# Token rows gathered as quarter rows and turned on VectorE in a mixture-of-experts block

## The reference

```
u = rms_norm(x);  proj = u @ w_in
h = x + concat(conv_group(proj), attention(q, k, v)) @ w_out    # 8 heads of 64, 2 key heads, 64-frame chunks
v = rms_norm(h, norm2_g)
logits = v @ router_w + router_b;  gates = softmax(top 4 of 32)
expert(e, v) = act @ w2[e] + b2[e],  act = clamped swiglu of (v @ w1[e] + b1[e])
y = h + sum over the token's 4 experts of gate * expert(e, v)
```

## Time and profile before

| | us |
|---|---|
| median of 3 runs (2012.42 to 2017.47) | 2012.59 |
| the profiled execution | 2012.99 |
| its span | 2011.3 |
| TensorE busy | 1948.9 |
| VectorE busy | 994.6 |
| ScalarE busy | 451.1 |
| GpSimd busy | 227.2 |

### The profile page before, as it was taken

The page is one execution under the profiler, slowest core; times in us unless marked ns, Lnnn a source line. Parts: engine busy times, 40 slices in busy tenths (PEclk is TensorE's granted clock), DMA queues, the critical chain, the costliest instruction groups (busy, mean ns, idle before and its releaser), DMA issues.

```text
span 2011.3 us, 35422 instructions
## 1 busy us (share of the span) xinstructions
PE 1948.9 (97%) x13245; PEld 1617.5 (80%) x13246; DVE 994.6 (49%) x2418; ACT 451.1 (22%) x983; POOL 227.2 (11%) x221
## 2 busy tenths in 40 slices
PE   5999999969999999999999999999999999999997
PEld 3555555438888778888877888999999999999996
DVE  3998972354554544454545454444444444343432
ACT  3265574121111111111111111222122211111111
POOL 3111100010001000101100110111111111100100
PEclk9999999979999999999999999999999999999998
DMA  6000035347999999999999998999888888887652
GB/s 240 1 1 1 24 81 182 133 177 281 330 322 344 335 343 344 341 314 341 345 334 343 343 335 307 316 315 302 295 294 296 299 303 301 287 283 250 215 181 44
DMA packets 233939, 509.08 MB, mean 253 GB/s; under 512 B 7997, under 2 KB 12633, under 8 KB 233888
## 3 DMA queue, kind: packets, MB, share of 16 engines
q1 hardware_dynamic: 215264, 447.97, 62.0%
q0 software_dynamic: 16768, 59.98, 10.8%
q10 hardware_dynamic: 1856, 0.41, 0.1%
HBM read 475.53 MB, written 32.80 MB: 253 GB/s over the span
## 4 chain that ended last, share of the span: by engine, by line
PE 93%; DVE 4%; ACT 1%; issue 1%; POOL 1%; DMA 1%; SPq 0%; ACTq 0%; DVEq 0%; POOLq 0%
PE bank L1138 49%; PE bank L1178 12%; PE bank L1153 12%; PE bank L1371 5%; PE bank L1249 5%; DVE arena L880 2%; PE bank L1517 2%; PE bank L1285 2%; PE bank L1296 1%; PE bank L1322 1%; PE bank L1166 1%; PE bank L1508 1%; PE bank L1167 1%; DMA arena<-in_x 1%; PE bank L1241 0%
## 5 line engine op out<-in xcount | busy, mean ns | idle before, releaser
L1138 PE MATMUL bank<-arena 128*128 128x128 f32 (+5 forms) x8192 | 993.7, 283 | 3.0 <-issue 2.9
L1138 PEld LDWEIGHTS bank<-arena 128*128 128x128 f32 x8192 | 984.9, 191 | 14.3 <-issue 13.7
L769 DVE TENSOR_SCALAR arena<-bank,b1c 128x256 f32<-128x256 f32 x256 | 123.8, 483 | 428.4 <-PE bank L1138 422.8
L469 ACT ACTIVATE arena<-arena 128x256 f32<-128x256 f32 x256 | 106.7, 417 | 849.8 <-DVE arena L769 768.4
L1178 PE MATMUL bank<-arena 128*128 128x512 f32 x576 | 262.1, 593 | 0.0
L1104 DVE TENSOR_SCALAR arena<-bank,cols 128x256 f32<-128x256 f32 x256 | 112.0, 479 | 295.1 <-PE bank L1517 295.1
L1153 PE MATMUL bank<-arena 128*128 128x144 f32 (+4 forms) x1792 | 246.0, 293 | 0.0
L1153 PEld LDWEIGHTS bank<-arena 128*128 128x128 f32 x1792 | 235.9, 190 | 0.1
L357 POOL DMA_INDIRECT out<-arena,idx_cur x64 | 99.0, 1547 | 855.9 <-DVE arena L819 846.1
L880 DVE SCALAR_TENSOR_TENSOR arena<-arena,cols 128x512 f32<-128x512 f32 (+1 forms) x226 | 182.3, 807 | 16.3 <-ACT arena L562 9.3
L1178 PEld LDWEIGHTS bank<-arena 128*128 128x128 f32 x576 | 102.5, 190 | 94.7 <-issue 94.7
(11 more groups left out here) (227 smaller groups left out, 1101.5 us busy)
## 6 DMA issues: line engine op xcount, KB each, us to landing
arena<-in_w SPq DMA_DIRECT2D x192, 2048.0 KB, 12.1
arena<-in_b SPq DMA_DIRECT2D x32, 512.0 KB, 11.0
arena<-in_x SPq DMA_DIRECT2D x16, 512.0 KB, 6.3
token_rows<-arena SPq DMA_DIRECT2D x8, 528.0 KB, 2.9
out<-arena SPq DMA_DIRECT2D x8, 512.0 KB, 6.0
arena<-in_w_in SPq DMA_DIRECT2D x2, 1536.0 KB, 13.0
arena<-in_w_in SPq DMA_DIRECT2D x1, 3072.0 KB, 19.5
arena<-in_w_out SPq DMA_DIRECT2D x1, 2048.0 KB, 7.8
```

What stands on the lines that cost most here:

```text
L469: a.activation(sg[:, m % 2, :], g1[:, m % 2, :], ACT.Sigmoid, scale=ALPHA).then_inc(sg_ready, 1)
L769: v.tensor_scalar(g1[:, r, :], bank[r][:, 0:SLOTS], b1c[:, m:m + 1], LIMIT, ALU.add, ALU.min).then_inc(g1_ready, 1)
L1138: last = mm(bank[m % 2][:, side * SLOTS:side * SLOTS + n], w1_sb[:, k, lo:lo + P], xT[:, k, 0:n], start=k == 0, stop=k == KD - 1)
```

## The change

The normalised row is stored with norm2_g already in it and with its features reordered, so that quarter q of the stored row holds features 32q to 32q+31 of each of the 8 feature blocks. The 32 gates go to a tensor of their own. In the passes, eight indirect DMAs fetch quarter rows of 1 KB: in DMA g, partition 32q + j receives quarter q of the token in slot 32g + j. VectorE then turns 32 x 32 blocks straight into `xT`; `trans_x`, its two PSUM banks' halves and `take_xT` go. The index of a quarter row is 4 x token + q, for which TensorE spreads the 256 token numbers over the partitions with one more float32 matmul of 8 columns per pass. The order of each pass changes with it. The first pass still takes whole rows and is turned by TensorE, after a ScalarE copy that undoes the reordering. The gates come by two more indirect DMAs of 128 rows of 128 bytes (`gather_gates`). In the attention, scores fill two banks at a time with heads of alternating groups. The last token tile's work is reordered, and `norm_v` on VectorE now takes all 8 tiles.

```diff
+BANK_PAIRS = ((0, 2), (1, 3))
-    rows_d = nc.dram_tensor("token_rows", [SEQ, ROW], f32, kind="Internal").ap()
+    rows_d = nc.dram_tensor("token_rows", [SEQ, D], f32, kind="Internal").ap()
+    quads_d = rows_d.rearrange("s (q c) -> (s q) c", q=4)
+    gates_d = nc.dram_tensor("token_gates", [SEQ, NE], f32, kind="Internal").ap()
...
 def store_rows(sp, t):
-            if t == NT - 1:
-                sp.wait_ge(v_ready, 1)
-            sp.dma_start(rows_d[t * P:(t + 1) * P, :], vrow[:, t % 2, :]).then_inc(row_out[t % 2], 16)
+            sp.dma_start(rows_d[t * P:(t + 1) * P, :], vrow[:, t % 2, 0:D]).then_inc(row_out[t % 2], 16)
+            sp.dma_start(gates_d[t * P:(t + 1) * P, :], vrow[:, t % 2, D:]).then_inc(row_out[t % 2], 16)
...
+            sp.dma_start(g2_row, norm2_g.rearrange("(o n) -> o n", o=1).to_broadcast([P, D])).then_inc(g2_in, 16)
...
+        def gather_quads(pool, n):
+            pool.wait_ge(idx_q_ready, n)
+            pool.sem_inc(pool_past, 1)
+            for g in range(8):
+                pool.indirect_dma_start(out=gath_q[:, g, :], out_offset=None, in_=quads_d,
+                                        in_offset=bass.IndirectOffsetOnAxis(ap=idx_q[:, g:g + 1], axis=0)
+                                        ).then_inc(quad_in, 16)
...
             with pool.Fori(0, n_pass) as q:
+                pool.wait_ge(xt_ev, q * 4 + 4)
+                gather_quads(pool, q + 1)
                 pool.wait_ge(cur_ready, q + 1)
-                pool.wait_ge(xt_mm, q * 4 + 4)
-                gather(pool, q + 2)
+                gather_gates(pool)
                 pool.wait_ge(y_ready, q + 1)
...
 def act_pass(a, q, over):
             with a.If(over < 1):
+                sigmoids()
                 take_rows(0)
                 take_rows(1)
             with a.Else():
+                sigmoids()
...
 # ScalarE, before the first pass
+                a.activation(first_tok[:, h, :].rearrange("p (k q r) -> p q k r", k=KD, q=4),
+                             gath[:, h, :].rearrange("p (q k r) -> p q k r", k=KD, q=4), ACT.Copy
+                             ).then_inc(first_tok_ready, 1)
...
 def dve_pass(v, q, e, e_next, prep, one_hots):
+            link(prep(rank[:, :, ds(e_next, 1)].rearrange("p t o -> p (t o)"), baseB[:, ds(q + 1, 1)]))
+            one_hots()
             hidden_a(0)
...
-                if m == 1:
-                    link(prep(rank[:, :, ds(e_next, 1)].rearrange("p t o -> p (t o)"), baseB[:, ds(q + 1, 1)]))
-                    one_hots()
+                if m == 2:
+                    v.wait_ge(idx_mm, q + 2)
+                    link(take_codes(v))
+                    link(take_idx(v, idxf[:]))
+                    link(v.tensor_copy(idx_pass[:], idx_next[:]))
+                    v.wait_ge(gate_in, q * 32 + 32)
+                    v.tensor_copy(idx_next[:], idxf[:]).then_inc(idx_ready, 1)
+                    v.tensor_tensor(spots[:], idxf[:].unsqueeze(2).to_broadcast([P, 2, 4]),
+                                    quad[:].unsqueeze(1).to_broadcast([P, 2, 4]), ALU.mult).then_inc(spots_ready, 1)
                 if m == 3:
+                    v.wait_ge(spread_mm, q + 1)
+                    v.tensor_scalar(idx_q[:], bank[6][:, 16:24], 4.0, quad_id[:], ALU.mult, ALU.add
+                                    ).then_inc(idx_q_ready, 1)
+                if m == 4:
                     for i in range(2):
                         v.wait_ge(added[i], q * 16 + 16)
...
             hidden_b(MT - 1)
-            for i in range(3):
-                take_xT(q4, i)
+            v.wait_ge(quad_in, q * 128 + 128)
+            for g in range(8):
+                ins = v.transpose(xT[:, :, g * 32:(g + 1) * 32], gath_q[:, g, :].rearrange("p (k r) -> p k r", k=KD))
+                if g % 2 == 1:
+                    ins.then_inc(xt_ev, 1)
...
 def norm_v(t):
-                v.tensor_scalar(vrow[:, t % 2, 0:D], hb[:, t % 4, :], rs[:, 2, t:t + 1], None, ALU.mult)
+                for g in range(4):
+                    v.scalar_tensor_tensor(dst[:, g], src[:, g], rs[:, 2, t:t + 1], gain[:, g], ALU.mult, ALU.mult)
...
 # VectorE, last tile
+            residual(NT - 1, (0,))
+            route(NT - 2)
+            residual(NT - 1, (1,))
+            v.wait_ge(lt_mm, NT - 1)
+            v.wait_ge(vt_mm, 2 * NT)
+            v.tensor_copy(vT[:, 4:8, :], bank[5][:].rearrange("p (k q) -> p k q", k=4)).then_inc(vt_ev, 1)
+            norm_v(NT - 1)
+            route(NT - 1)
...
 def pe_pass(pe, q, n, slots_to_tokens):
-                        if m == 0 and side == 0 and k % 2 == 0:
-                            pe.wait_ge(xt_ev, q4 - 3 + k // 2)
+                        if m == 0 and side == 0 and k == 0:
+                            pe.wait_ge(xt_ev, q4)
+                if m == 1:
+                    slots_to_tokens(q + 2)
                 if m == 3:
-                    slots_to_tokens(q + 2)
+                    pe.wait_ge(spots_ready, q + 1)
+                    mm(bank[6][:, 16:24], copies[:], spots[:].rearrange("p h g -> p (h g)"), start=True,
+                       stop=True).then_inc(spread_mm, 1)
...
 def scores(s):
-                for b in range(4):
-                    if s >= 1 and b < 3:
-                        pe.wait_ge(pt_ev, 3 * (s - 1) + b + 1)
-                    if s >= 1 and b == 3:
-                        pe.wait_ge(o_ev, s)
-                    for h in (2 * b, 2 * b + 1):
+                for pair in BANK_PAIRS:
+                    if s >= 1:
+                        if pair == BANK_PAIRS[0]:
+                            pe.wait_ge(pt_ev, 3 * s)
+                        else:
+                            pe.wait_ge(o_ev, s)
+                    for i in range(2):
+                        for b in pair:
+                            g, j = divmod(2 * b + i, GROUP)
...
 # TensorE, last tile
+            out_half(NT - 1, 0)
+            turn_rows(NT - 2)
+            fold_logits(NT - 3)
+            out_half(NT - 1, 1, (0,))
+            logits(NT - 2)
+            out_half(NT - 1, 1, (1,), range(2))
+            turn_rows(NT - 1, (0,))
+            fold_logits(NT - 2)
+            out_half(NT - 1, 1, (1,), range(2, CT))
+            turn_rows(NT - 1, (1,))
+            logits(NT - 1)
```

More of the change, by code:

```diff
@@ L465, in act_pass, with sigmoids @@
             q2 = a.snap(q * 2)
[L466 to L469, removed]
+            def sigmoids():
+                for m in range(MT):
+                    a.wait_ge(g1_ready, q8 + m + 1)
+                    a.wait_ge(sg_free, q8 + m + 1)
+                    a.activation(sg[:, m % 2, :], g1[:, m % 2, :], ACT.Sigmoid, scale=ALPHA).then_inc(sg_ready, 1)
             def take_yT(d):
@@ new lines, in turn_rows @@
+            def turn_rows(u, sides=(0, 1)):
+                if u == 0:
+                    pe.wait_ge(cn_done, 2 * CT)
+                if u == 1:
+                    pe.wait_ge(o_ev, NT)
+                for b in sides:
+                    if u >= 1:
+                        pe.wait_ge(vt_ev, 2 * u)
+                    pe.wait_ge(h_ready if b else h_half, u + 1)
+                    for k in range(4):
+                        c = 4 * b + k
+                        last = pe.transpose(bank[4 + b][:, k * P:(k + 1) * P], hb[:, u % 4, c * P:(c + 1) * P], ident[:])
+                    last.then_inc(vt_mm, 1)
@@ new lines, in logits @@
+            def logits(u):
+                pe.wait_ge(vt_ev, 2 * u + 2)
+                if u >= 1:
+                    pe.wait_ge(lg_neg, u)
+                for j in range(2):
+                    for g in range(4):
+                        last = mm(bank[6][g * NE:(g + 1) * NE, 0:P], rw[:, 4 * j + g, :], vT[:, 4 * j + g, :],
+                                  start=j == 0, stop=j == 1)
+                last.then_inc(lt_mm, 1)
+            for t in range(NT - 1):
+                if t >= 2:
+                    out_half(t, 0)
+                if t >= 1:
+                    turn_rows(t - 1)
+                if t >= 2:
+                    fold_logits(t - 2)
+                if t == 0:
+                    pe.wait_ge(mix_ready, CT)
+                if t == NT // 2:
+                    pe.wait_ge(mix_ready, 2 * CT)
+                out_half(t, 1)
@@ L1473, in _ @@
                     out_half(1, 0, (1,))
-                if 1 <= t <= NT:
-                    u = t - 1
-                    pe.wait_ge(vt_ev, 2 * u + 2)
-                    if u >= 1:
-                        pe.wait_ge(lg_neg, u)
-                    for j in range(2):
-                        for g in range(4):
-                            last = mm(bank[6][g * NE:(g + 1) * NE, 0:P], rw[:, 4 * j + g, :], vT[:, 4 * j + g, :],
-                                      start=j == 0, stop=j == 1)
-                    last.then_inc(lt_mm, 1)
+                else:
+                    logits(t - 1)
                 if t == 1:
@@ L1510, in slots_to_tokens @@
                 last.then_inc(idx_mm, 1)
-            def trans_x(before, i, halves=2):
```

(13 more changed lines are left out.)

218 lines of the change are left out of this document (87 added, 131 removed).

## The result

| | us |
|---|---|
| changed kernel, median of 4 runs (2170.01 to 2175.86) | 2172.84 |
| before, median of 4 runs (2012.42 to 2017.47) | 2014.90 |
| ratio, 95% interval | 1.0784 (1.0771 to 1.0797) |
| profiled execution of the changed kernel, span | 2173.15, 2171.4 |

What follows compares the result with a forecast made beforehand. TensorE was taken as the bound, busy for 97% of the span. Terms -40.9 + 6.9 + 0.4 + 0.3 + 2.7 - 6.0 = -36.6 took 2012.99 to 1976.4 us, 1976 for the median; range 1967 to 1993.

Steps and rivals of the forecast that it cites:

- The quarter gathers: GpSimd's extra gathers and VectorE's transposes in each pass: `xT` complete 5.5 us early, so no cost.
- Rival (d): Quarter rows arrive late and narrow passes wait; at 3.0 us between issues +112, 2088 us; chance 0.05.
- Row transposes and spreading matmul in narrow passes: TensorE in passes: transposes leave, 0.11 us each (-40.9 in all); two new instructions add 0.108 each (+6.9).
- The spots' round trip: VectorE-TensorE-VectorE wait before the spreading matmul: margin 0.7 us, no cost; as a rival +16, 1992 us, chance 0.11.
- DMA (c): DMA traffic in passes: same bytes, more and smaller packets, gates adding 0.4 us, which fits into 2.3 idle.
- rival (c): DMA engines become the bound through 93 ns small packets: +39 over 18 narrow passes, 2015 us; chance 0.10.
- wide passes: TensorE's passes with four row transposes: these take 0.44 us of the chain between down matmuls, all counted as gain.
- Scores: Attention scores: alternating row halves overlap, -0.85 us in each of seven tiles, -6.0 in all.
- rival (a): Score matmuls in the attention don't overlap, so their 6 us gain is lost: 1982 us; chance 0.14.
- Last tile: Last token tile: `norm_v(7)` stands ahead of `route(7)`, which starts at 429.9 instead of 427.16: +2.7 us.
- Constants: VectorE's constants before the convolution: five more short operations, partly inside its waits: +0.3 us, bounds 0 and 1.0.
- The bounds: Lower and upper limits of all the forecast's terms together: said to span 1968 to 1985 us.

Runs made afterwards that it cites:

- e1_pairs: Changed kernel with the eight quarter gathers sent two at a time and the gate gathers held back: 1995.72 us, ratio 0.9903.
- g1_best: Changed kernel, quarter gathers in two rows of four, gate gathers held back, three down-projection banks in wide passes, last-tile row and constants rearranged: 1986.64 us.
- s1: Kernel before with only the alternating order of the scores: 2011.71 us, ratio 0.9988.
- h1: Kernel before with six computing instructions on GpSimd behind the two gathers of each pass: 2016.71 us, ratio 1.0005.
- e4: Kernel before with six more gathers of 32 bytes a row behind the two of each pass: 2051.77 us, ratio 1.0177.
- h2: The kernel of e4 run again, on chip 4, against the kernel before: 2058.47 us, ratio 1.0211.
- r4: The kernel of e8 run again, on chip 5, beside a stalling control: 2240.42 us, ratio 1.1115.
- e8: Changed kernel with each quarter gather fetching for 16 partitions instead of 128, on chip 3: 1990.53 us, ratio 0.9883.
- f2: Changed kernel with the two gate gathers of a pass fetching for 16 partitions instead of 128: 2210.98 us, ratio 1.0974.
- f1: Changed kernel with the two gate gathers behind a wait for TensorE's hidden tile 6 of the pass: 2092.58 us, ratio 1.0383.

## Why the prediction was wrong

**The step that failed** is "The quarter gathers ... Cost of all this: nothing, cover 5.5 us a pass". I counted the six more DMAs and their landing as a deadline for `xT`, and put GpSimd down as an engine that is only late or on time. I did not ask what eight issues in a row do to the others. It is 1720.1 us from the first pass's start to the end in the changed kernel and 1541.1 in e1_pairs (2171.4 - 451.29; 1990.8 - 449.66): **179.0 of the 196.7 us** missed (179.0 here, 13.3 in the passes without the stall, -20.3 for -33.6, and 4.4 ahead of them). Of these 179, TensorE's idle time in the passes is 84 (94.2 against 10.0). The clock was at half for 141 us of the passes instead of 5. TensorE was busy for some 125 of them, so that costs about 60. The rest, some 35, fits matmuls that come singly: 0.27 us for one (782.02 in the changed kernel's chain), where they take 0.11 each in a row. Rival (d), quarters late, had the direction and not the mechanism: the issues stayed 1.24 to 1.33 us apart.

The rest of the steps, read in e1_pairs, where the stall is away:

- **Row transposes and spreading matmul in narrow passes**: 43.69 to 43.03, as forecast. The spreading matmul's 0.22 is 0.12 of its own and 0.10 in the matmuls behind it (14.39 in e1 for the 128 that took 14.29). The spots' round trip cost nothing.
- **DMA (c)**: the traffic cost nothing either, but the count of packets was wrong. The forecast had 1024 packets of 1 KB in the place of 256, and 256 for the gates, so 1024 more a pass; q0 has 5184 more in all, 162 a pass. In the trace the eight quarter gathers of a pass are 256 packets of 4096 bytes. That q0's time grows by the forecast's 0.4 us a pass (10.6% of 2171.4 against 10.8% of 2011.3) is luck, and rival (c), priced by 1024 small packets, had no ground here.
- **In wide passes** I had 16 x 0.11 - 0.22 = -1.5 and got -0.63 to -0.92 (51.31 to 50.55 for 144 slots). The chain of that pass of e1_pairs (L1216 is the down projection, L514 takes its result), against the earlier trace rows:

```profile
1403.65 3.69 PE bank L1216 x30
...
1407.36 0.39 ACT arena L514
...
1407.80 2.23 PE bank L1216 x16
...
1421.62 0.24 issue
1421.87 0.39 PE bank L1197
```

  The transposes had covered ScalarE's taking of a PSUM bank (0.46 of the chain) and the step into the next pass (0.24). I had named no cover for them: some 10 us over 14 passes. In g1_best the third bank removes the first of the two; the same stretch of the next pass, also of 144 slots, is

```profile
1451.29 5.88 PE bank L1235 x48
```

  and that pass takes 50.0 us.
- **The end**: 18.3 us from the last matmul to the end of the span (1972.5 to 1990.8) where it was 15.0 (1996.3 to 2011.3). Of the 3.3 more, 0.5 lie before the last two indirect adds and the rest behind them. No run was made for this, but the traces bear on it. From the last add to the end of the span it is 8.0 to 8.3 us in the kernel before, s1 and h1, and 11.1 to 11.8 with ten gathers of 128 rows a pass. It is 12.3 and 12.9 with the six tiny ones of e4 and h2 added to the two of before, and 8.3 to 9.1 where a pass's quarter or gate gathers were cut to 16 rows (r4, e8, f2). So it hangs on the gathers; how is open.
- **Scores**: -0.85 a tile was forecast. A block's 16 instructions take 1.63 us of the chain instead of 2.25, so -0.62. The tiles of s1, with only the order of the scores changed, are shorter by the same 0.63; its time agrees with -4.4 but can't tell it from much less. An instruction takes 0.10 instead of 0.14, so halves overlap, in part only: rival (a) is out.
- **Last tile**: `route(7)` starts behind `norm_v(7)`, which ends at 428.43 where the route had begun at 427.16, with all before it 1.2 us earlier: +2.5 against +2.7.

```profile
427.16 1.27 DVE arena L1039 x3
428.43 0.24 DVE lg L1044
...
451.29 1.86 PE bank L1192 x7
```

- **Constants**: the first projection block starts at 104.78 instead of 103.83, 0.95 against 0.3. In all, the first pass starts at 451.29 where the forecast of the front gives 446.9 (449.93 + 0.3 + 2.7 - 6.0), 4.4 late. The runs with the same front reach it anywhere from 448.91 (r4) to 454.80 (e8), so this term is no finer than that.
- **The bounds**: taken all one way, those of the terms give 1967 to 1989, not 1968 to 1985.

The rule of "SBUF — State Buffer" in the Trainium skill, that VectorE in a two-port mode can hold up GpSimd's descriptor writing, was not tested. From 771.66 to 773.4 VectorE works without a pause, and the issues beside it are 1.28 to 1.33 us apart, 1.24 to 1.26 without it; but two of these four operations read PSUM and two have two inputs, and no run tells whether any was in such a mode. The harm went another way, from GpSimd's issues to TensorE.

**Left open.** Which path TensorE's signals and instructions share with GpSimd's issues; whether other long work on GpSimd does the same (h1 was too short); and why the runs of chip 3 were free of it, which may be the chip or something else in that session, as the changed kernel itself was not run there. Loading of code by DMA is out: the changed kernel's trace has no packet of the instruction queues (q8, q14) between 495 and 1355 us, where all narrow passes but the first lie. That eight quarter gathers for 16 partitions do more harm than for 128 fits the closer spacing of the issues (1.16 us instead of 1.25), but was not tested apart.

## What to carry to other kernels

Count the indirect DMAs that GpSimd issues in one row, not only their bytes: here, on three of the four chips named, up to four at a time beside a dense float32 matmul stream were free and eight cost 4 us a pass; waits that split the row of ten were worth 8%. When "issue" stands as the reason for a TensorE gap and the next engine's idle says "remote", look at what GpSimd does at that time. And before taking filler out of a bound engine's queue, look which waits it had covered.

## What was not expected of the hardware

- TensorE's signals reached VectorE up to 6.5 us late in a row of 8 to 10 indirect DMA issues (f2_gates16), up to 8.3 with quarter gathers of 16 rows (r4_rows16), and GpSimd too (2.56 us idle in f1); otherwise 0.04 us behind the last matmul.
- TensorE went on with hidden matmuls for 8.3 us from the row's first issue (7.3 in r4, 8.7 in f1), then one to four came at a time.
- After that TensorE's granted clock was 0.50 for up to 6.8 us, in which it was mostly busy; about a third of the loss is this.
- The stall is not there on every chip, or in every session: three kernels that ran at 1991 to 1996 us on one chip took 2090 to 2240 on another, while the kernel before ran at 2013 to 2017 on all.
